# A two-layer hybrid encoder on one core: the projection's weight remainders computed by VectorE, sigmoids by log and exp, and feed-forward norms multiplied in behind the products

## The reference, cut to what matters

```
x = x + 0.5 * swiglu(rmsnorm(x, n1), f1g, f1u, f1d)          # first feed-forward part, width 2816
z = rmsnorm(x, nm) @ w_in                                     # 31 blocks of 128 output columns
logf = log_sigmoid(ff + b_f)
o_fox  = softmax attention with forgetting (logf) * sigmoid(fg)
o_rwkv = rwkv_mix(z_rwkv): token shift, a = sigmoid(a0 + ad @ a_up),
         decay = exp(-exp(-0.5) * sigmoid(w0 + tanh(wd) @ w_up)), g = sigmoid(gd) @ g_up, state recurrence
o_ret  = head_norm(retention(q, k, v)) * silu(g)
x = x + concat(o_fox, o_rwkv, o_ret) @ w_out
x = x + 0.5 * swiglu(rmsnorm(x, n2), f2g, f2u, f2d)           # second feed-forward part
x = x + sigmoid(x @ w_ple_gate) * rmsnorm(p @ w_ple_proj, pn)

rmsnorm(x, g) = x * rsqrt(mean(x*x) + 1e-6) * g
swiglu(h, wg, wu, wd) = (silu(h @ wg) * (h @ wu)) @ wd
```

## Time and profile before

| | |
|---|---|
| median of three runs | 1607.78 us |
| profiled execution, whole time | 1615.51 us |
| its span | 1614.0 us |
| TensorE busy | 1501.8 us (93%) |
| VectorE, ScalarE, GpSimd busy | 861.7, 593.5, 195.2 us |
| mean granted TensorE clock | 0.925 of full |
| moved from and to memory | 129 GB/s over the span |

### The profile page before, as it was taken

One profiled execution on the slowest core, in us unless ns is written; L12 is line 12 of the kernel. 1 busy time (PEld: TensorE's weight loads), 2 busy tenths in 40 slices (PEclk: granted clock), 3 DMA queues, 4 the chain that ended last, 5 costly groups with the idle time before them and its releaser, 6 DMA issues. The chain is left out here.

```text
span 1614.0 us, 27287 instructions
## 1 busy us (share of the span) xinstructions
PE 1501.8 (93%) x11228; PEld 1420.6 (88%) x11228; DVE 861.7 (53%) x1238; ACT 593.5 (37%) x871; POOL 195.2 (12%) x129
## 2 busy tenths in 40 slices
PE   7999999978988999999979999998889889999997
PEld 6999989967766899999979999897777578999997
DVE  4555344787545345553555553448684633555535
ACT  4334334431123443332443342343411335334333
POOL 1000016641020000000000000175500200000000
PEclk9999999978777999999989999999885779999999
DMA  7444433321010334444334444243300122444443
GB/s 303 159 157 173 165 130 130 135 97 61 5 67 31 138 142 160 159 175 162 135 136 156 162 174 159 105 156 131 123 12 11 60 79 105 156 158 175 162 160 134
DMA packets 32035, 209.76 MB, mean 130 GB/s; under 512 B 4392, under 2 KB 6072, under 8 KB 7752
## 3 DMA queue, kind: packets, MB, share of 16 engines
q1 hardware_dynamic: 29392, 200.34, 34.1%
q0 software_dynamic: 2560, 8.26, 1.5%
HBM read 204.49 MB, written 4.10 MB: 129 GB/s over the span
## 5 line engine op out<-in xcount | busy, mean ns | idle before, releaser
L797 DVE TENSOR_TENSOR split_w<-wc,split_w 128x2048 fp32r<-128x2048 f32 x140 | 320.6, 2292 | 374.2 <-ACT split_w L524 374.2
L524 ACT ACTIVATE split_w<-wc 128x2048 fp32r<-128x2048 f32 x140 | 268.3, 1916 | 541.6 <-PE bank L1261 341.6
L1255 PE MATMUL bank<-split_x,split_w 128*128 128x288 f32 x2816 | 398.7, 299 | 15.8 <-ACT split_x L530 15.8
L1255 PEld LDWEIGHTS bank<-split_x,split_w 128*128 128x128 f32 x2816 | 385.6, 190 | 20.8 <-issue 13.2
L1278 PE MATMUL bank<-split_x,split_w 128*128 (+1 forms) x2112 | 282.2, 295 | 0.0
L1278 PEld LDWEIGHTS bank<-split_x,split_w 128*128 128x128 f32 x2112 | 281.8, 188 | 0.0
L1261 PE MATMUL bank<-split_x,split_w 128*128 128x288 f32 x1408 | 202.2, 296 | 0.3 <-DVE split_w L797 0.3
L1261 PEld LDWEIGHTS bank<-split_x,split_w 128*128 128x128 f32 x1408 | 192.6, 189 | 0.5 <-DVE split_w L797 0.5
L424 POOL TENSOR_TENSOR split_x<-wc,split_x 128x1024 fp32r<-128x1024 f32 x32 | 78.1, 2440 | 514.2 <-ACT split_x L568 514.2
L568 ACT ACTIVATE split_x<-wc 128x1024 fp32r<-128x1024 f32 x62 | 65.4, 1058 | 112.3 <-PE bank L1332 112.3
L1329 PE MATMUL bank<-split_h,split_x 128*128 128x288 f32 x496 | 84.3, 313 | 7.4 <-ACT split_h L573 7.4
(11 more groups left out here) (285 smaller groups left out, 1624.7 us busy)
## 6 DMA issues: line engine op xcount, KB each, us to landing
wc<-wcol SPq DMA_DIRECT2D x174, 1024.0 KB, 4.8
wc<-wfirst SPq DMA_DIRECT2D x12, 1024.0 KB, 4.8
con<-consts_in SPq DMA_DIRECT2D x1, 2182.0 KB
arena<-kc_in POOLq DMA_DIRECT2D x8, 256.0 KB, 3.2
arena<-vc_in POOLq DMA_DIRECT2D x2, 1024.0 KB, 5.1
xT<-x_in SPq DMA_DIRECT2D x2, 576.0 KB, 4.5
k_out<-zT POOLq DMA_DIRECT2D x8, 144.0 KB, 2.2
v_out<-zT POOLq DMA_DIRECT2D x8, 144.0 KB, 2.4
```

What stands on the lines that cost most here:

```text
L524: act.activation(ws[s % 2][0], wc[:, p % RING, :], ACT.Copy).then_inc(S["cast"], 1)
L797: dve.tensor_tensor(lo, wc[:, (POS_FFN[f] + s) % RING, :], hi, ALU.subtract).then_inc(S["wlo"], 1)
L1255: pe.matmul(o, hi[:, k, cs], x[:, k, :], start=(w == 0 and k == 0), stop=False)
```

## The change

1. In the projection VectorE computes the weights' `lo` parts (`z_rest`) in place of GpSimd, at 31 fixed places between its RWKV steps. The two loops over blocks are written out, and TensorE, ScalarE and VectorE have a new order there: ScalarE copies the finished block first and casts the next weights after it.
2. The sigmoids of the decay, the `a` factor, the small group and the retention gate are computed as exp(-log(1 + e)) by ScalarE (`sigmoid_of`), after VectorE has cut `e` at 2 to the 60 (`at_most`), in place of the reciprocals on VectorE. The forgetting group's gates keep the reciprocal.
3. In both feed-forward parts x is split with the gain alone (`first_part`, `second_part`), before its norm is known. The factor `rs` is multiplied onto the gate product (`half`) before the tanh, and onto the product after up, two more pairs of VectorE instructions for two blocks. The first round of each loop is written out.
4. The mean of squares there is one matmul in slot 1 over squares that VectorE has summed first (`sum_of`), in place of eight matmuls ahead of the part. So it is with the mean of the product of `p`, and with the final norm, which is now made in the last block of the program. The first norm no longer exists ahead of the first layer.
5. In the first slot of each feed-forward part the product with `lo` weights comes before the one with `lo` activations. One buffer of the output product's weights moves.

```diff
                     def ffn(f):
                         if f == 0:
                             rest(0, 0)
+                            for b in range(DB):
+                                second_part(0, b)
+                            dve.wait_ge(first_sem["sq"], DB)
+                            sum_of(hT, "sqsum")
                             rest(0, 1)
...
+                    def sum_of(sq, done):
+                        link(dve.tensor_tensor(sq[:, 0:4, :], sq[:, 0:4, :], sq[:, 4:8, :], ALU.add))
+                        link(dve.tensor_tensor(sq[:, 0:2, :], sq[:, 0:2, :], sq[:, 2:4, :], ALU.add))
+                        dve.tensor_tensor(sq[:, 0, :], sq[:, 0, :], sq[:, 1, :], ALU.add).then_inc(S[done], 1)
+                    def second_part(f, b):
+                        dve.wait_ge(S["h_hi"], DB * f + b + 1)
+                        dve.scalar_tensor_tensor(h_lo[:, b, :], xT[:, b, :], pa(("n1", "n2")[f], b), h_hi[:, b, :],
+                                                 ALU.mult, ALU.subtract).then_inc(S["h_lo"], 1)
...
                             rest(f, 2 * jj + 2, i)
+                            for q in (2 * jj, 2 * jj + 1):
+                                dve.wait_ge(S["gate_ps"], i * 4 + (FB * f + q + 1))
+                                dve.tensor_tensor(half[:, q % 2, :], bank[2 * (q % 4)][:, 0:T], rs[:], ALU.mult)\
+                                   .then_inc(S["half"], 1)
...
+                            for q in (2 * jj, 2 * jj + 1):
+                                dve.wait_ge(S["raw"], i * 4 + (FB * f + q + 1))
+                                dve.tensor_tensor(e, e, rs[:], ALU.mult).then_inc(S["hidden"], 1)
...
-                    def rest(n, i=0):
-                        pool.wait_ge(S["zcast"], i * 8 + n + 1)
-                        pool.tensor_tensor(lo, z_raw(n), hi, ALU.subtract).then_inc(S["zlo"], 1)
+                    def z_rest(n):
+                        dve.wait_ge(S["zcast"], n + 1)
+                        if n >= 2:
+                            dve.wait_ge(S["z_ps"], n - 1)
+                        dve.tensor_tensor(lo, z_raw(n), hi, ALU.subtract).then_inc(S["zlo"], 1)
...
+                    def first_part(f, b):
+                        act.wait_ge(S["x_ready"], 16 * f + b + 1)
+                        act.activation(h_hi[:, b, :], xT[:, b, :], ACT.Copy, scale=pa(("n1", "n2")[f], b)).then_inc(S["h_hi"], 1)
...
+                    def sigmoid_of(e, done):
+                        link(act.activation(e, e, ACT.Ln, bias=col(C_ONE)))
+                        return act.activation(e, e, ACT.Exp, scale=-1.0).then_inc(S[done], 1)
...
+                                    if begin and s == 1:
+                                        pe.wait_ge(S["sqsum"], f + 1)
+                                        pe.matmul(bank[5][:, 0:T], c("mean"), hT[:, 0, :], start=True, stop=True)\
+                                          .then_inc(S["norm_ps"], 1)
...
-                    norm(2)
-                    pe.wait_ge(S["x_ready"], 24)
...
-                    for b in range(DB):
-                        pe.wait_ge(S["pj_sq"], b + 1)
-                        mm = pe.matmul(bank[7][:, 0:T], c("mean"), proj_sq[:, b, :], start=(b == 0), stop=(b == DB - 1))
-                    mm.then_inc(S["pn_ps"], 1)
-                    pe.wait_ge(S["ple_rs"], 1)
                     ffn(1)
```

More of the change, by code:

```diff
@@ L95 @@
 LOG_DECAY = -float(np.exp(-0.5))
+EXP_MOST = float(2.0 ** 60)
 def head_of(g):
@@ L262, in program @@
         E = Space(arena, ARENA)
-        squares = (None, hT, E.take(DB, T), hT)
+        ple_gate = E.take(DB, T)
+        half = hT[:, 0:2, :]
         proj_sq = E.take(DB, T)
@@ L611, in _ @@
                                        bias=negp[:, i:i + 1]).then_inc(S["e_low"], 1)
-                    z_slot(9)
+                    z_block(11)
+                    for i in range(2):
+                        act.wait_ge(S["most"], 2 + i)
+                        sigmoid_of(sig4[:, 2 * i:2 * i + 2, :], "sig_low")
+                    z_block(12)
                     for b in range(2):
@@ L901, in _ @@
                     dve.tensor_tensor(fe[e8, :], fe[e8, :], fu[e8, :], ALU.min).then_inc(S["fu_ok"], 1)
+                    z_rest(11)
+                    z_rest(12)
+                    lw, aa = sig4[:, 0:2, :], sig4[:, 2:4, :]
+                    for i in range(2):
+                        dve.wait_ge(S["e_low"], 2 * i + 2)
+                        at_most(sig4[:, 2 * i:2 * i + 2, :])
+                    z_rest(13)
+                    dve.wait_ge(S["sig_low"], 1)
+                    for b in range(2):
+                        dve.tensor_tensor_scan(lc[:, b, :], c("restart"), lw[:, b, :], 0.0,
+                                               ALU.mult, ALU.add).then_inc(S["lcs"], 1)
@@ L904, in _ @@
                        .then_inc(S["lgf_ok"], 1)
+                    for b in range(2):
+                        dve.wait_ge(S["rgate"], b + 1)
+                        at_most(rgt[b])
                     dve.wait_ge(S["lgf_ok"], 1)
@@ L957, in _ @@
[L957 to L967 removed]
+                    z_rest(23)
@@ L1347, in low_rank, with rotate @@
                                   rhs, start=True, stop=True).then_inc(S["low_ps"], 1)
+                    def rotate(b):
+                        pe.matmul(bank[4 + b % 2][:, 0:T], c("rot"), zT[:, Z_TQ + b, :], start=True, stop=True)\
+                          .then_inc(S["rot_ps"], 1)
+                    for n in range(11):
+                        z_block(n)
+                    pe.wait_ge(S["lowin"], 1)
                     for i in range(4):
                         low_rank(i)
-                    z_slot(0, 9)
+                    z_block(11)
+                    z_block(12)
                     pe.wait_ge(S["e_low"], 4)
@@ L1358, in _ @@
                           .then_inc(S["kk_ps"], 1)
-                    for s in range(10, 12):
-                        z_slot(0, s)
-                    def rotate(b):
-                        pe.matmul(bank[4 + b % 2][:, 0:T], c("rot"), zT[:, Z_TQ + b, :], start=True, stop=True)\
-                          .then_inc(S["rot_ps"], 1)
+                    for n in range(13, 17):
+                        z_block(n)
                     pe.wait_ge(S["kln"], 2)
@@ L1770, in _ @@
                        .then_inc(end_sem["y"], 1)
+            @block.tensor
+            def _(pe):
+                pe.wait_ge(end_sem["norm"], 3)
+                pe.matmul(bank[0][:, 0:T], c("mean"), hT[:, 0, :], start=True, stop=True).then_inc(end_sem["norm"], 1)
+            @block.scalar
+            def _(act):
+                act.wait_ge(end_sem["norm"], 4)
+                act.activation(rs[:], bank[0][:, 0:T], ACT.Ln, bias=col(C_EPS)).then_inc(end_sem["norm"], 1)
+                act.wait_ge(end_sem["norm"], 5)
+                act.activation(rs[:], rs[:], ACT.Exp, scale=-0.5).then_inc(end_sem["norm"], 1)
             @block.sync
```

408 lines of the change are left out of this document (219 added, 189 removed).

## The result

The changed kernel takes 1556.19 us (median of 4 runs, 1555.32 to 1557.50) against 1607.76 us (4 runs, 1605.37 to 1614.41) for the kernel before on the same chip: a ratio of 0.967, 95% interval 0.964 to 0.970. The forecast was 1559, 1544 to 1582.

What follows compares the result with a forecast made beforehand. TensorE, which never waits in the loops, was taken to bound the kernel. 2 x (-2.5 - 13.9 - 9.4) - 2.0 + 1.7 + 2.9 = -49.0 us from profiled 1615.5, less 7.7 for the median: 1559, range 1544 to 1582.

Steps and rivals of the forecast that it cites:

- The projection: Projection's body: 119.9 to 106 us, -13.9 a layer; block 23's wait goes as reciprocal and scans no longer precede the keys.
- The projection's start: Norm and first block of each projection: TensorE starts earlier, -2.5 us a layer; at half clock the gain is 1.8 smaller.
- The second feed-forward part's start: From the output product's end to slot 1: 25.7 us before, 15.3 after, means 1.0 in slot 1; -9.4 us a layer.
- The loop: Feed-forward loops: four more VectorE instructions for two blocks, 1.7 us, and TensorE still doesn't wait: 0.
- The start of the program: Before the first layer: TensorE again starts at about 16.3 us, cold first slot 10.4 us, mean +0.5: +1.7 us.
- The mixers: Mixers between the projection and the output product: their products are the same before and after, so no change.
- The turn: Turn to the second layer: ScalarE and TensorE start earlier, the single mean costs 0.5: -2.0 us, once.
- the end: Final norm in the last block: barrier ends 1.7 us earlier, then sums, cold matmul, ln and exp take 4.5: +2.9 us.
- Rival C: Projection's three short waits bring TensorE's clock to half, three falls a layer of about 3.4 us: 20 us, 1579; 15%.
- D: Rival: no waits in the projection's body (-7 us) and full clock at its start (-5): 1547; 18%.
- F: Rival: B and Rival C together, plus stalls behind ScalarE's late casts, take back the gain: 1605; 3%.
- B: Rival: VectorE's long times in the projection are its own and subtractions stand behind them; 12 us a layer more, 1583; 7%.

Runs made afterwards that it cites:

- the run with two additions: The changed kernel with two idle 1728-column additions on VectorE ahead of each pair's product with rs in both feed-forward parts: 1574.32 us, ratio 0.977.

## Why the prediction came out right, step by step

The time was right to 3 us, but in part by luck. The steps summed to -49.0, and the profiles differ by 58.0. The median of the runs gave 6.4 of these 9 us back, because the execution of the kernel before that had been profiled was a long one. Of the 9 us, 5.8 are the mixers and 4.2 the start of the program; the projection gave 2.2 less than forecast.

- **The projection.** Shown. Forecast 106 us for the body, measured 105.74; waits at blocks 9, 16 and 25 forecast as 1.4, 0.9 and 1.2 us, measured 1.05, 0.39 and 1.16. Their removal shortens the body by 3.2 us, to 102.5, where I had 3.5 and 102.3. The premise, VectorE's short times without GpSimd, is what the run with the subtractions put back isolates. The reason I gave for the missing wait at block 23, the reciprocal, is not borne out in the new order: with the reciprocals back, the waits in both layers grow by 1.0 us in all. The engine of the subtractions brings 25.7 of 30.7 us, and how much of the other 5.0 is the new order was not tested. The rule of the Trainium skill (SBUF — State Buffer, Who interferes with whom) that I leaned on agrees with the rows: 2.33 us for seven columns with two inputs, beside a subtraction of 2.40. The instruction of seven columns with one input, which took 2.26 us, the rule as I quoted it does not cover.
- **The projection's start.** -1.5 us in the first layer against -2.5: the case "half clock still hits this start" came, which I had put at 1.8 less and which cost 1.0. TensorE started 1.5 us earlier against the mean's start, and its first block took 7.7 us where I had 6.8 (7.6 in the kernel before). It was idle for 2.19 us ahead of the first product and then paced by the eight norm products; eight matmuls at 239.84 take 2.04 us against 1.23 in the steady body. The norm itself is 3.52 us, as forecast.
- **The second feed-forward part's start.** -9.85 against -9.4. The wait for the last copy is 0.50, not 1.0:

```profile
532.76 10.93 PE L1333 MATMUL bank<-split_x,split_w 128*128 128x288 f32 x80 [0.50 <-ACT extra L749]
543.52 0.65 PE L1318 MATMUL bank<-hT,con 128*128 128x288 f32 x2
544.01 0.65 PE L1322 MATMUL bank<-arena,con 128*128 128x288 f32 x2
```

  The two single means take 0.76 us (543.52 to 544.28) and lengthen the part from slot 1 on by 0.9, against the 1.0 I gave them.
- **The loop.** 0, as forecast; the slack is at least the 3.9 us of the run with two additions.
- **The start of the program** is the step that failed: "the first cast waits for its weights, which the dropped norm only filled, so TensorE again starts at about 16.3". It starts at 11.87. The cast does wait for its weights in the changed kernel, but they land at 9.33 us. In the kernel before they had landed at 9.54, and I had read the 0.41 us between the barrier and the cast at 14.04 as their arrival. So the dropped norm had not filled a wait; it had been the wait. +1.7 should have been -2.5: 4.56 earlier, a slot 0 of 10.7 us instead of 9.05, and a mean. That slot was forecast at 10.4 as a cold one, and it is: the pace is that of the lower level until 19.8, with ScalarE's parts of x pacing the first eight matmuls.
- **The mixers**, put at no change, gave 2.8 and 3.0 us. Their instructions and order are the same. The difference is the clock: it went up at another place among them. In the second layer, eight products of the kernel before and of the one after:

```profile
1258.66 4.20 PE L1596 MATMUL bank<-arena,con 128*128 128x288 f32 x8
```
```profile
1209.06 2.21 PE L1670 MATMUL bank<-arena,con 128*128 128x288 f32 x8
```

  The granted clock over these very stretches:

```profile
1258.66:1262.86 4.20, 4.20 (x12) 2.95 (x11) 2.48 (x6) 0.00 (x0) 2.20 (x4) 0.52 0.38 117
```
```profile
1209.06:1211.27 2.21, 2.21 (x14) 1.74 (x11) 2.00 (x6) 0.00 (x0) 0.60 (x2) 1.00 0.00 0
```

  Over all fourteen profiles the stretch from the mixers' first transpose to the product of `p` (less the 3.9 us of the mean where it is there) takes 174.2 to 179.7 us in a layer; in the changed kernel's two profiles 176.2 to 176.9. I have no run that steers it, and what sets the place stays open. The two layers of one profile can differ by 2.6 us (179.25 and 176.65 us with the feed-forward parts alone changed), so I count it as luck.
- **The turn** gave 2.8 for 2.0, **the end** cost 3.4 for 2.9: the cold matmul takes 1.33 us for its two passes, not 0.8.

Rival C (three falls of the clock) did not come: the clock stood at 1.00 throughout the body, in spite of three waits of at most 1.16 us. Its other half, the clock at the projection's start, did. D had the waits away and full clock at the start, 1547; the kernel with the waits removed, the last sum moved and the turn warmed runs at 1546.7 (a ratio of 0.959, which is 1542 in the units of the forecast), without that full clock. F would have needed B and C.

## What to carry to other kernels

Price an engine by what it does to its neighbours: GpSimd's 2.39 us subtractions had slack of their own, and cost 25.7 us (in the new order of the steps) by making VectorE's instructions wait for them, the shortest as much as the long ones. Where an engine is loaded to 59% and the order of its work is fixed, look at each late instruction and move it ahead of one that is not waited for so soon; three such moves brought 6 us. Before saying that an instruction at a stage's start waits for its data, look for a barrier in front of it and compare the time at which the data landed: the same 0.41 us of idle time stood ahead of a cast whose weights had been there for 4.5 us, and ahead of one that started 0.05 us behind them.

## What the runs showed of the hardware that I had not expected

- The exclusion between VectorE and GpSimd showed both ways and on tiny instructions: a 128x7 `tensor_scalar` with one input took 2.26 us beside GpSimd against 0.17 alone, and a GpSimd subtraction 3.56 against 2.40.
- At the projection's start TensorE waited for 2.19 us and then did eight matmuls paced by the norm. The granted clock stood at 1.00 through the wait and fell to 0.50 at about 234.8, 0.8 us into these matmuls (in the second layer 0.1 us ahead of them). TensorE ran at its lower level (1.2 GHz) until 241.6; the granted clock is 0.75 over the stretch of 13.91 us, so half of full for about 7 of them. Three waits of 0.4 to 1.2 us between full blocks left it at the upper level.
- A granted clock of 1.00 in the first 20 us of a profile can be the lack of a record. The distance between matmuls of 288 columns tells the level: 0.24 us at the lower, 0.133 at the upper.
- Same instructions, same order, up to 5.5 us apart in one layer's mixers and output product. In the two compared above the granted clock changed level at another place.
- The end of a block of the program costs: in the changed kernel ScalarE ends its last square at 1541.38 and loads, until 1542.69, the table for the final norm's logarithm; the first sum of the final block, which VectorE makes and which needs no table, starts at 1544.70, 2.0 us later.
